# Latent up-projections of queries, keys and values as three products of rounded parts

## The reference, cut to what matters

```python
c_q = rmsnorm(q_lat, P['mla_q_norm'][l])                 # 384 wide
qa = (c_q @ P['w_mla_uq'][l]).reshape(b, t, H_A, A_NOPE + A_ROPE)
c_kv = rmsnorm(kv_lat, P['mla_kv_norm'][l])              # 256 wide, a cache row of the output too
kv = (ckv_all @ P['w_mla_ukv'][l]).reshape(b, -1, H_A, A_NOPE + A_V)
```

## Time and profile before

| | |
|---|---|
| three runs | 3065.31, 3065.8, 3066.28 us |
| the profiled execution, its own time | 3065.62 us |
| its span, first to last instruction | 3063.8 us |
| busy: TensorE, VectorE, GpSimd, ScalarE | 2984.9, 1501.9, 1064.9, 1031.6 us |
| mean granted TensorE clock | 0.992 of full |

### The profile page before, as it was taken

How to read it: one execution, slowest core, us unless ns; L and a number is a source line. 1 busy time by engine, 2 the same in 40 slices (tenths; PEclk the granted TensorE clock), 3 DMA queues, 4 the chain that set the end, 5 groups by cost and what they waited for, 6 DMA issues and landing times.

```text
span 3063.8 us, 54011 instructions
## 1 busy us (share of the span) xinstructions
PE 2984.9 (97%) x23006; PEld 2755.8 (90%) x23006; DVE 1501.9 (49%) x1818; ACT 1031.6 (34%) x1743; POOL 1064.9 (35%) x517
## 2 busy tenths in 40 slices
PE   9999998999999999999999999999999999999998
PEld 8999996956888999999999999879467889999998
DVE  4555162854345455553265542536543454655523
ACT  3222243363445242222232222432634452422221
POOL 3334333312232434344433344323031324343342
PEclk9999999999999999999999999999999999999999
DMA  4222263111111222222222212322021113222222
GB/s 156 90 89 71 76 147 117 59 48 59 53 59 60 93 99 97 82 87 76 85 97 86 92 59 93 124 101 71 22 74 48 66 55 125 82 83 84 81 81 72
DMA packets 46108, 252.67 MB, mean 82 GB/s; under 512 B 6224, under 2 KB 8368, under 8 KB 30064
## 3 DMA queue, kind: packets, MB, share of 16 engines
q1 hardware_dynamic: 40000, 232.63, 21.4%
q0 software_dynamic: 5840, 17.50, 2.3%
q10 hardware_dynamic: 96, 0.08, 0.0%
HBM read 234.33 MB, written 15.85 MB: 82 GB/s over the span
## 4 chain that ended last, share of the span: by engine, by line
PE 90%; ACT 4%; DVE 3%; issue 2%; DMA 1%; DVEq 0%; SPq 0%; ACTq 0%
PE PS L726 36%; PE PS L731 18%; PE PS L1130 14%; PE PS L736 4%; PE PS L627 2%; PE PS L1311 2%; PE PS L910 1%; PE PS L972 1%; PE PS L1099 1%; PE PS L1287 1%; DMA ring<-in_w_vb 1%; PE PS L839 1%; PE PS L1032 1%; PE PS L1251 1%; PE PS L1256 1%
## 5 line engine op out<-in xcount | busy, mean ns | idle before, releaser
L457 POOL TENSOR_TENSOR ring_r<-ring,piece_h 128x1024 fp32r<-128x1024 f32 (+1 forms) x228 | 601.1, 2636 | 961.3 <-ACT piece_h L1432 961.3
L1432 ACT ACTIVATE piece_h<-ring 128x1024 fp32r<-128x1024 f32 (+1 forms) x228 | 262.7, 1152 | 1112.7 <-PE PS L731 1108.4
L457 POOL TENSOR_TENSOR ring_r<-ring,piece_m 128x1024 fp32r<-128x1024 f32 (+1 forms) x156 | 331.6, 2131 | 799.2 <-ACT piece_m L1432 798.9
L726 PE MATMUL PS<-u_l,piece_h 128*128 128x272 f32 x2624 | 543.0, 288 | 0.0
L726 PE MATMUL PS<-uT_r,piece_h 128*128 128x272 f32 x2624 | 542.5, 288 | 0.0
L731 PE MATMUL PS<-uT_r,ring_r 128*128 128x272 f32 x3040 | 412.0, 288 | 0.0
L726 PEld LDWEIGHTS PS<-uT_r,piece_h 128*128 128x128 f32 x2624 | 410.8, 188 | 0.4
L726 PEld LDWEIGHTS PS<-u_l,piece_h 128*128 128x128 f32 x2624 | 411.0, 188 | 0.0
L731 PEld LDWEIGHTS PS<-uT_r,ring_r 128*128 128x128 f32 x3040 | 392.6, 188 | 0.0
L1863 DVE TENSOR_TENSOR rstd<-rstd,sq 128x544 f32<-128x544 f32 x34 | 106.4, 3131 | 349.3 <-ACT sq L1355 349.1
L726 PE MATMUL PS<-act_l,piece_h 128*128 128x272 f32 x1232 | 255.8, 290 | 0.0
(11 more groups left out here) (311 smaller groups left out, 4948.4 us busy)
## 6 DMA issues: line engine op xcount, KB each, us to landing
ring<-in_w_up SPq DMA_DIRECT2D x88, 1024.0 KB, 4.8
ring<-in_w_dn SPq DMA_DIRECT2D x64, 704.0 KB, 4.2
ring<-in_w_mg SPq DMA_DIRECT2D x48, 768.0 KB, 4.1
ring<-in_w_in SPq DMA_DIRECT2D x22, 1024.0 KB, 4.8
ring<-in_w_out SPq DMA_DIRECT2D x8, 1024.0 KB, 4.8
x_spill<-xT SPq DMA_DIRECT2D x2, 2176.0 KB, 19.6
xT<-x_spill SPq DMA_DIRECT2D x2, 2176.0 KB, 8.8
ring<-in_w_vb SPq DMA_DIRECT2D x8, 512.0 KB, 8.9
```

The costliest lines, as they stand in the source:

```text
L457: nc.gpsimd.tensor_tensor(ring_r[:, ch[0] % NSLOT, at:at + n], w, hi, ALU.subtract).then_inc(S["w_low"], 1)
L726: mm(PS[:, 2 * u + b, 0:HALF], w, x[k][:, HALF * b:HALF * b + HALF], start=first and k == 0 and n == 0, stop=False)
L1432: A(buf[:, hs, 0:n], ring[:, ch % NSLOT, at:at + n], ACT.Copy).then_inc(S["w_high"], 1)
```

## The change

GpSimd splits the normalised latents `ql` and `ckv` into rounded and remaining parts, right behind the last row outputs, while branch B runs. The three or two low parts go in place of the source; for `ckv` that waits for the row outputs. ScalarE rounds six pieces of the up-projection weights: two inside branch B, behind steps 12 and 16, four between the evacuations of the query tiles. GpSimd makes their low parts, two ahead of the wait for `sb_out` and four spread through the splitting of branch B's output. TensorE makes each product from three rounded ones. The last value tile is computed for 128 keys, of which ScalarE copies the 32 new ones. The counters of pieces shift by six per layer (`N_G` in place of `N_IN` for the gate and output weights; these lines are left out).

```diff
+N_LAT = 6
+N_G = N_IN + N_LAT
+PC_MIX = N_G + 48 + 8
...
+LAT_PIECES = [(16, 0, 768), (16, 768, 768), (17, 0, 768), (17, 768, 768), (18, 0, 1024), (19, 0, 1024)]
...
+        ql_h, ql_l = region_r("ql_h", 30280, KQ, TOK), region_r("ql_l", 15920, KQ, TOK)
+        ckv_h = [region_r("ckv_h0", 31912, NKEY), nc.alloc_sbuf_tensor_at("ckv_h1", [P, NKEY], F32R, offset=x_at + 4 * TOK)]
+        ckv_l = region_r("ckv_l", 14320, KKV, NKEY)
...
+                def lat_low(i):
+                    ch, at, n = LAT_PIECES[i]
+                    low(l, PC_M, N_IN + i, (CH_M + ch, i % 2), at, n)
+
+                for k in range(KQ):
+                    nc.gpsimd.tensor_copy(ql_h[:, k, :], ql[:, k, :]).then_inc(S["lat_split"], 1)
+                for k in range(KQ):
+                    pool.wait_ge(S["lat_split"], l * 10 + k + 1)
+                    nc.gpsimd.tensor_tensor(ql_l[:, k, :], ql[:, k, :], ql_h[:, k, :].bitcast(F32), ALU.subtract).then_inc(S["lat_split"], 1)
+                for k in range(KKV):
+                    nc.gpsimd.tensor_copy(ckv_h[k][:], ckv[:, k, :]).then_inc(S["lat_split"], 1)
+                pool.wait_ge(S["rows_out"], 16 * (l * 12 + 12))
+                for k in range(KKV):
+                    pool.wait_ge(S["lat_split"], l * 10 + 6 + k + 1)
+                    nc.gpsimd.tensor_tensor(ckv_l[:, k, :], ckv[:, k, :], ckv_h[k][:].bitcast(F32), ALU.subtract).then_inc(S["lat_split"], 1)
+                lat_low(0)
+                lat_low(1)
                 pool.wait_ge(S["sb_out"], l * 5 + 5)
-                split(1, qB, 0)
+                lat_low(2)
+                for k in range(4):
+                    nc.gpsimd.tensor_copy(o_h[1][:, k, :], qB[:, k, :]).then_inc(S["split"], 1)
+                lat_low(3)
+                for k in range(4):
+                    pool.wait_ge(S["split"], l * 16 + k + 1)
+                    nc.gpsimd.tensor_tensor(o_l[1][:, k, :], qB[:, k, :], o_h[1][:, k, :].bitcast(F32), ALU.subtract).then_inc(S["split"], 1)
+                lat_low(4)
+                lat_low(5)
                 gate_low(0)
                 branch_low(0)
...
-                pe.wait_ge(S["lat_ready"], l * 7 + 3)
+                def latent_tile(name, piece, at, x_h, x_l, n):
+                    t, K = TILE[name], len(x_h)
+                    u, (slot, w_at, _) = t % 2, LAT_PIECES[piece]
+                    w_l = ring_r[:, (ch + slot) % NSLOT, w_at + at:w_at + at + K * P]
+                    open_tile(l, u, T_M + t // 2)
+                    pe.wait_ge(S["w_high"], lat + piece + 1)
+                    for k in range(K):
+                        for x in (x_h[k], x_l[k]):
+                            for b in range(2):
+                                mm(PS[:, 2 * u + b, 0:n], piece_m[:, piece % 2, at + k * P:at + k * P + P], x[:, n * b:n * b + n],
+                                   start=k == 0 and x is x_h[0], stop=False)
+                    pe.wait_ge(S["w_low"], lat + piece + 1)
+                    for k in range(K):
+                        for b in range(2):
+                            ins = mm(PS[:, 2 * u + b, 0:n], w_l[:, k * P:k * P + P], x_h[k][:, n * b:n * b + n], start=False, stop=k == K - 1)
+                    ins.then_inc(done[u], 1)
+
+                pe.wait_ge(S["lat_split"], l * 10 + 6)
                 for i in range(8):
-                    w = chunk(l, ch + 16 + i // 4)
-                    at = (i % 4) * KQ * P
-                    tile(TILES[27 + i], [(w[:, at + k * P:at + k * P + P], ql[:, k, :]) for k in range(KQ)])
+                    latent_tile(TILES[27 + i], i // 2, (i % 2) * KQ * P, [ql_h[:, k, :] for k in range(KQ)], [ql_l[:, k, :] for k in range(KQ)], HALF)
                     if i == 0:
                         sample_values(l)
...
+                w_l = ring_r[:, (ch + 19) % NSLOT, 0:1024]
+                pe.wait_ge(S["w_high"], lat + 6)
+                pe.wait_ge(S["w_low"], lat + 6)
                 for i, kts in enumerate(VA_KEYS):
...
                     for b, kt in enumerate(kts):
-                        m = P if kt < 6 else NEW
+                        at = P * kt if kt < 6 else NKEY - P
                         for k in range(KKV):
-                            ins = mm(PS[0:m, 2 * u + b, :], ckv[:, k, P * kt:P * kt + m], w[:, k * 512:k * 512 + 512],
-                                     start=k == 0, stop=k == KKV - 1)
+                            w = slice(512 * k, 512 * k + 512)
+                            mm(PS[:, 2 * u + b, :], ckv_h[k][:, at:at + P], piece_m[:, 1, w], start=k == 0, stop=False)
+                            mm(PS[:, 2 * u + b, :], c_l[k][:, at:at + P], piece_m[:, 1, w], start=False, stop=False)
+                            ins = mm(PS[:, 2 * u + b, :], ckv_h[k][:, at:at + P], w_l[:, w], start=False, stop=k == KKV - 1)
...
                 for i in range(4):
+                    if i % 2:
+                        filled(l, unit_of(f"uq{i}"), turn_of(f"uq{i}"))
+                        high_in(N_IN + 2 + i // 2)
                     to_queries(f"uq{i}", qAn[:, i, :])
...
+                for g in range(2):
+                    filled(l, unit_of(f"qs{g}"), turn_of(f"qs{g}"))
+                    high_in(N_IN + 4 + g)
...
                     if v >= 7 and v % 4 == 3:
                         out_pair((v - 7) // 4)
+                    if v in (12, 16):
+                        high_in(N_IN + (v - 12) // 4)
```

More of the change, by code:

```diff
@@ L71 @@
 N_IN = 27
-PC_MIX = N_IN + 48 + 8
+N_LAT = 6
+N_G = N_IN + N_LAT
+PC_MIX = N_G + 48 + 8
 PC_A, PC_M, PC_B = 0, PC_FFN, PC_FFN + PC_MIX
@@ L145 @@
 OUT_PIECES = [(44 + i // 2, (i % 2) * 1024, 1024) for i in range(KD)]
-PIECE_OF = {t: i for i, t in enumerate(TILES[:6])} | {t: 10 + i for i, t in enumerate(LATE_TILES)} | {f"wo{n}": N_IN + 48 + n for n in range(KD)}
+PIECE_OF = {t: i for i, t in enumerate(TILES[:6])} | {t: 10 + i for i, t in enumerate(LATE_TILES)} | {f"wo{n}": N_G + 48 + n for n in range(KD)}
+LAT_PIECES = [(16, 0, 768), (16, 768, 768), (17, 0, 768), (17, 768, 768), (18, 0, 1024), (19, 0, 1024)]
+assert len(LAT_PIECES) == N_LAT
 V_DONE = {f"V{i}": i + 1 for i in range(V_CHUNKS - 1)}
@@ L161, in build @@
         PS = ctx.enter_context(nc.psum_tensor("PS", [P, 8, 512], F32))
+        x_at = (nc.sbuf_base + 31) // 32 * 32
         xT = sb("xT", [P, KD, TOK])
@@ L546, in gate_low @@
                 def gate_low(m):
-                    low(l, PC_M, N_IN + 2 * m, (CH_M + 20 + m, 0), 0, 1024)
+                    low(l, PC_M, N_G + 2 * m, (CH_M + 20 + m, 0), 0, 1024)
                 def branch_low(m):
-                    low(l, PC_M, N_IN + 1 + 2 * m, (CH_M + 20 + m, 1), 1024, 512)
-                pool.wait_ge(S["sb_out"], l * 5 + 5)
-                split(1, qB, 0)
+                    low(l, PC_M, N_G + 1 + 2 * m, (CH_M + 20 + m, 1), 1024, 512)
+                def lat_low(i):
[14 more added lines that the diff above has]
+                lat_low(1)
+                pool.wait_ge(S["sb_out"], l * 5 + 5)
+                lat_low(2)
[7 more added lines that the diff above has]
+                lat_low(5)
                 gate_low(0)
@@ L583, in _ @@
                 for n, (ch, at, m) in enumerate(OUT_PIECES):
-                    low(l, PC_M, N_IN + 48 + n, (CH_M + ch, n % 2), at, m)
+                    low(l, PC_M, N_G + 48 + n, (CH_M + ch, n % 2), at, m)
                 ffn(l, PC_B, CH_B)
@@ L1010, in mixer @@
                 branch_b(l)
-                pe.wait_ge(S["lat_ready"], l * 7 + 3)
+                lat = l * PC_LAYER + PC_M + N_IN
+                def latent_tile(name, piece, at, x_h, x_l, n):
[14 more added lines that the diff above has]
+                    ins.then_inc(done[u], 1)
@@ L1020, in mixer @@
-                w = chunk(l, ch + 18)
+                pe.wait_ge(S["lat_split"], l * 10 + 10)
+                c_l = [ckv_l[:, k, :] for k in range(KKV)]
                 for i in range(4):
-                    tile(f"kA{i}", [(w[:, (i * KKV + k) * P:(i * KKV + k + 1) * P], ckv[:, k, :]) for k in range(KKV)],
-                         n=(0, NKEY // 2, NKEY))
-                w = chunk(l, ch + 19)
+                    latent_tile(f"kA{i}", 4, i * KKV * P, [ckv_h[k][:] for k in range(KKV)], c_l, NKEY // 2)
@@ L1106, in merge_span @@
                 b = MERGES[m][0]
-                piece = l * PC_LAYER + PC_M + N_IN + 2 * m
+                piece = l * PC_LAYER + PC_M + N_G + 2 * m
                 w_l = ring_r[:, (CH_M + 20 + m) % NSLOT, :]
@@ L1519, in high_in @@
                         high(CH_M + ch, 0, i % 2, at, n, l, piece_f if i in (4, 5) else piece_m)
-                    elif N_IN + 48 <= i < N_IN + 48 + KD:
-                        ch, at, n = OUT_PIECES[i - N_IN - 48]
+                    elif N_IN <= i < N_G:
+                        ch, at, n = LAT_PIECES[i - N_IN]
+                        high(CH_M + ch, 0, (i - N_IN) % 2, at, n, l)
+                    elif N_G + 48 <= i < N_G + 48 + KD:
+                        ch, at, n = OUT_PIECES[i - N_G - 48]
```

(7 more changed lines are left out.)

5 lines of the change are left out of this document (2 added, 3 removed).

## The result

The changed kernel takes **3071.76 us**, median of 18 runs, against 3066.11 for the kernel before in 18 runs of the same measurement: ratio 1.0019, interval 1.0012 to 1.0026. One of the 18 runs took 4475.28 us at a mean granted clock of 0.596; ratio and interval are those of the other 17. Forecast were 11 us less; it came out 5.65 us slower, and the interval does not hold 1. The profiled execution took 3070.89 us with a span of 3068.8, against 3065.62 and 3063.8.

The account below looks back on a forecast made before the run. TensorE was taken to bound the product stage, with a ScalarE-TensorE round ahead in branch B. Per layer -8.4 + 1.0 + 1.8 = -5.6 us, twice -11.2, from 3065.8 to 3054.6 us; range 3049.0 to 3061.0.

Parts of the forecast that it names:

- Part 1: Product stage on TensorE: three rounded products replace each full one, 36.9 us in place of 45.31, 8.4 us less per layer.
- the fourth rival: Product stage: rounded products cost a quarter of a full one, saving 11.3 us per layer before waits; 3048.8 us, chance 0.03.
- Part 2: ScalarE's six weight roundings per layer, two in branch B and four in the product stage, hide in its waits: cost nothing.
- Part 4: GpSimd's queue in the product stage makes TensorE stall 0 to 2.7 us at the first key tile, taken as 1.8.
- Part 3: Branch B: VectorE's two-operand additions collide with GpSimd's splitting, costing 0 to 3.3 us per layer, taken as 1.0.
- the addition at 713.08: VectorE addition beside GpSimd's subtractions before the change: 1.64 us against 0.69 alone; its 0.95 wait priced branch B's collision.
- No change of clock enters the sum: TensorE's granted clock in the products is 1.00 of full, 2.4 GHz, so the forecast has no clock term.
- The third, an unserved queue: VectorE served only when GpSimd's queue rests: +8.4 us in branch B, +11 in the product stage per layer; 3088, chance 0.06.

Follow-up runs that it names:

- the last kernel: Changed kernel with GpSimd's latent splitting put behind branch B's additions, plus low part of key weights made before the last two output subtractions: 3048.01 us, ratio 0.9933.
- the run moved: Changed kernel with GpSimd's latent splitting cut in two, each part waiting until a head pair's two additions in branch B are done: 3052.74 us, ratio 0.9950.
- The kernel with the rest: Changed kernel with one wait for VectorE's first softplus of branch B ahead of GpSimd's ten latent instructions: 3057.59 us.

## Why the prediction was wrong, point by point

- **Part 1, the products: right.** Query tiles follow at 2.25 us (the third and the fourth rounding, two tiles apart, start at 717.03 and 721.52; forecast 2.27), key tiles at 1.46 + 0.74 = 2.20 (2.2), values from 741.0 to 750.78 in 9.8 (9.8). A rounded product of 400 columns costs 2.20 / 12 = 0.183 us, the straight line's value. In layer 1 of the last kernel, where the stall is gone, the product stage is 8.37 us shorter than before: the 8.4 by itself. A quarter of the full product's price, the fourth rival, did not happen.
- **Part 2, the roundings: right.** They delay no tile, and with the run moved branch B is as long as before though two of them stand in it. The third (717.03) stands at the head of GpSimd's queue that ends in the stall, and part 4 had counted its time there.
- **Part 4, GpSimd in the product stage: right.** The queue is in the order that was worked out, 8 us later since branch B ended 8.1 later, and 1.7 more by the end of the key piece (733.40); the one stall is at the first key tile, where TensorE's records leave 1.52 us idle; forecast 1.8, between ends of 0 and 2.7. The product stage is 6.6 us shorter, as -8.4 + 1.8 gives.
- **Part 3, the collision in branch B: wrong, 9.7 instead of 1.0, and outside its ends of 0 and 3.3.** The step that failed is the sentence on the addition at 713.08: "it waited 0.95 and was then served, though more subtractions were queued". It was taken as how GpSimd and VectorE meet everywhere. The row is from the product stage, where the run is not behind a DMA issue. In branch B the run stands directly behind two of them, its instructions overlap by 0.2 us, and the addition waited to its end. The kernel with the rest shows what the step would have been worth without that: +1.3 and +1.2, near the 1.0. The places were right: the first of the two additions, its way over TensorE to ScalarE, and no slack there; so was the mark that was set for part 3 being wrong, branch B longer by over 3 us.
- **TensorE's clock was not in the sum.** "No change of clock enters the sum" was read in the products and holds there in the changed kernel (1.00 from 709.69 on). But the wait itself brought 0.53 behind it and 2.2 us per layer. This second term was put at nothing; the 9.7 is 7.5 of waiting and this.
- **The rivals.** The third, an unserved queue, had the mechanism but for both stages alike: its price of 8.4 in branch B was near (7.5 of waiting), its 11 in the product stage did not appear. That its price was near is in part luck: it had nothing on what stands ahead of the run. A rival with the first part alone, -8.4 + 1.8 + 8.4 per layer, twice 1.8, would have given 3069.4 us, 3.6 over the kernel before where 5.65 were measured. It was missing, because one row was made to speak for both stages.

The Trainium skill (SBUF — State Buffer, Summary: rules for kernel authors) says that, where VectorE reads two inputs from SBUF while GpSimd's instruction reads SBUF, the second one to issue blocks until the first finishes. The runs agree where GpSimd has rested (waits of 0.42 to 0.74 us, the rest of one instruction). Behind a DMA issue the wait was longer than that: 7.5 us, for the instruction then running and the five queued behind it.

## What to carry to other kernels

A collision on a port is to be priced at the place where it will happen, with what stands ahead of it in the queue: the same addition beside the same run waited 0.4 to 0.7 us where the run started from a rest and 7.5 where it stood behind a DMA issue. Work that is put on an idle engine is best placed by what its neighbours do not need just then; two waits moved the run into such gaps and turned a loss of 5.65 us into a gain of 15, and one piece brought forward made it 20. Where an engine that feeds TensorE waits for many microseconds, the low granted clock behind the wait belongs into the sum.

## What was not expected of the hardware

A run of GpSimd instructions directly behind GpSimd's own DMA issue overlaps itself by 0.2 us from instruction to instruction, and VectorE's addition of two SBUF operands took 8.1 to 8.6 us in place of 0.69 (0.76 as two halves), up to the run's end, in all five kernels that have this order. A nop between changes nothing; a wait of 0.74 or 1.04 us does, and so does the run ahead of the DMA issue: there the overlap is 0.06 us and the wait 0.4 to 0.7. That the overlap keeps VectorE out fits every run; what in the engine makes it was not shown. A granted clock of 0.53 followed TensorE's wait of 7.3 us, and cost 2.2 us; in the other kernels with this wait it cost 1.7 to 2.2.
